# A hybrid block whose second-norm rows are turned in 32x32 squares by VectorE and placed by DMA

## The reference, cut to what matters

```python
x = x + jnp.einsum('bse,ed->bsd', y, w_out[l])

h = rmsnorm(x, norm_ffn[l])
f = jax.nn.silu(jnp.einsum('bsd,df->bsf', h, w_gate[l])) * jnp.einsum('bsd,df->bsf', h, w_up[l])
x = x + jnp.einsum('bsf,fd->bsd', f, w_down[l])
return rmsnorm(x, norm_final)
```

## Time and profile before

| | |
|---|---|
| median of 3 runs | 1905.11 us (1903.91 to 1905.77) |
| span of the profiled execution | 1902.7 us (the profile gives no time beyond it) |
| PE busy | 1875.1 us, 99% |
| DVE, ACT, POOL busy | 1106.6, 808.4, 1144.9 us |
| mean granted clock of PE | 0.996 |
| DMA queue of SP | 283.25 MB, 44.8% of 16 engines |

### The profile page before, as it was taken

One profiled execution on the slowest core, in us unless ns is written; L12 is line 12 of the kernel. 1 busy time (PEld: TensorE's weight loads), 2 busy tenths in 40 slices (PEclk: granted clock), 3 DMA queues, 4 the chain that ended last, 5 costly groups with the idle time before them and its releaser, 6 DMA issues.

```text
span 1902.7 us, 22499 instructions
## 1 busy us (share of the span) xinstructions
PE 1875.1 (99%) x8374; PEld 1544.2 (81%) x8374; DVE 1106.6 (58%) x1269; ACT 808.4 (42%) x938; POOL 1144.9 (60%) x427
## 2 busy tenths in 40 slices
PE   9999999999999999999999999999999999999998
PEld 7888788877788788888888788888888888888886
DVE  6899988997645755455545854445443025433535
ACT  6466766585643533333333433333333222232235
POOL 3577477945734465666655755555555676676663
PEclk9999999999999999999999999999999999999999
DMA  6222132265777334533355433323333765655455
GB/s 196 78 79 88 45 100 78 75 224 172 247 240 231 117 125 127 153 119 127 112 153 176 151 105 114 106 88 105 115 105 127 288 225 190 210 189 211 166 198 221
DMA packets 240946, 284.20 MB, mean 149 GB/s; under 512 B 12095, under 2 KB 166207, under 8 KB 240364
## 3 DMA queue, kind: packets, MB, share of 16 engines
q1 hardware_dynamic: 240874, 283.25, 44.8%
q10 hardware_dynamic: 2, 0.00, 0.0%
HBM read 200.90 MB, written 82.31 MB: 149 GB/s over the span
## 4 chain that ended last, share of the span: by engine, by line
PE 82%; POOL 6%; DVE 5%; ACT 2%; issue 2%; DMA 2%; POOLq 0%; SPq 0%; DVEq 0%; ACTq 0%
PE ps L2133 19%; PE ps L2135 19%; PE ps L2134 19%; PE acc L2133 8%; PE acc L2135 8%; PE acc L2134 8%; DVE a_lo L1863 1%; POOL nsq L877 1%; PE ps L2161 1%; DVE t_sum L1887 1%; POOL nsq L879 1%; POOL w_lo L804 1%; POOL f_lo L1018 0%; DVE wo_lo L1707 0%; POOL glu L827 0%
## 5 line engine op out<-in xcount | busy, mean ns | idle before, releaser
L933 POOL TENSOR_TENSOR t_lo<-t_sum,t_hi 128x2048 fp32r<-128x2048 f32 x44 | 205.6, 4674 | 165.3 <-ACT t_hi L1366 165.2
L927 POOL TENSOR_TENSOR b_lo<-m_raw,b_hi 128x1536 fp32r<-128x1536 f32 x44 | 157.6, 3582 | 179.2 <-ACT b_hi L1361 121.9
L1018 POOL TENSOR_TENSOR f_lo<-f_raw,f_hi 128x2048 fp32r<-128x2048 f32 (+1 forms) x42 | 182.2, 4338 | 129.3 <-ACT f_hi L1518 124.8
L2133 PE MATMUL ps<-h_hi,w_hi 128*128 128x512 f32 x512 | 201.1, 393 | 0.8 <-POOL w_lo L804 0.8
L2135 PE MATMUL ps<-h_hi,w_lo 128*128 128x512 f32 x512 | 199.4, 389 | 0.0
L2134 PE MATMUL ps<-h_lo,w_hi 128*128 128x512 f32 x512 | 199.2, 389 | 0.0
L1887 DVE TENSOR_TENSOR t_sum<-m_raw 128x512 f32<-128x512 f32 x88 | 141.7, 1630 | 97.4 <-PE acc L2135 87.6
L1518 ACT CAST f_hi<-f_raw 128x2048 fp32r<-128x2048 f32 (+1 forms) x42 | 74.3, 1769 | 263.6 <-PE ps L2135 168.1
L2133 PE MATMUL ps<-wd_hi,f_hi 128*128 128x512 f32 x462 | 179.8, 389 | 0.8 <-POOL wd_lo L1025 0.8
L2134 PE MATMUL ps<-wd_lo,f_hi 128*128 128x512 f32 x462 | 179.7, 389 | 0.0
L2135 PE MATMUL ps<-wd_hi,f_lo 128*128 128x512 f32 x462 | 179.7, 389 | 0.0
(11 more groups left out here) (257 smaller groups left out, 4689.1 us busy)
## 6 DMA issues: line engine op xcount, KB each, us to landing
f_raw<-f_scr SPq DMA_DIRECT2D x35, 1024.0 KB, 4.9
wd_raw<-in_w_down SPq DMA_DIRECT2D x60, 512.0 KB, 6.6
f_scr<-fs SPq DMA_DIRECT2D x110, 256.0 KB, 2.1
m_raw<-in_w_gate SPq DMA_DIRECT2D x88, 256.0 KB, 3.9
m_raw<-in_w_up SPq DMA_DIRECT2D x88, 256.0 KB, 5.1
w_raw<-in_w_in SPq DMA_DIRECT2D x32, 512.0 KB, 5.3
f_scr<-gt SPq DMA_DIRECT2D x44, 256.0 KB, 2.0
xt<-in_x SPq DMA_DIRECT2D x16, 512.0 KB, 6.3
```

The lines of the kernel that those rows point to most:

```text
L927: g.tensor_tensor(b_lo[b][:, :, :, :], m_raw[b][:, 0:3], f32(b_hi[b][:, :, :, :]), ALU.subtract).then_inc(s_mlo, 1)
L933: g.tensor_tensor(t_lo[b][:, :, :, :], t_sum[b][:, :, :, :], f32(t_hi[b][:, :, :, :]), ALU.subtract).then_inc(s_mlo, 1)
L1018: g.tensor_tensor(f_lo[j % 3][:, 0:n], f_raw[j % 2][:, 0:n], f32(f_hi[j % 3][:, 0:n]), ALU.subtract).then_inc(s_dlo, 1)
L2133: pe.matmul(bank, lhs[0](c), rhs[0](c), start=first, stop=False, skip_group_check=more)
```

## The change

PE turns nothing any more. DVE's `transpose` turns each 32x32 square of the row in place: 16 instructions `row_turned`, from `hn` into `h2t`. That leaves the squares in the wrong places: square (t, b), for positions 32t to 32t+31 and channels 32b to 32b+31, has its channels on partitions 32t to 32t+31. Four DMAs per row, one for each 32 partitions, bring the squares to their places in DRAM in pieces of 32 numbers (128 B). ACT's queue issues them (`store_h2`), where SP's issued one DMA per row with pieces of 512 B. `h2_scr` has a new layout, and so each load of a quarter is four loads of 32 partitions with pieces of 2 KB as before (`load_quarter`; the quads likewise). `h2t` has four buffers for the first eight rows. DVE waits for a buffer's stores before it turns into it again; ACT waits for the turn before it issues.

```diff
-    h2_scr = nc.dram_tensor("h2_scr", [NH, P, KD, HALF], F32).ap()
+    h2_scr = nc.dram_tensor("h2_scr", [NH, SQ, KD, SQS, HALF], F32).ap()
...
-            def store_h2(w):
-                h, i = divmod(w, TPH)
-                sp_.wait_ge(s_h2c, 2 * (w + 1))
-                sp_.dma_start(h2_scr[h, :, :, i * P:(i + 1) * P], h2t[w % 2][:, :, :]).then_inc(s_h2st[w % 2], 16)
...
+            def load_quarter(n, h, a, done):
...
+                for q in range(SQS):
+                    sp_.dma_start(a_raw[n][q * SQ:(q + 1) * SQ],
+                                  h2_scr[h, :, half * KH:(half + 1) * KH, q, st * TILE:(st + 1) * TILE]).then_inc(done, 16)
...
-            def h2_copy(w):
-                if w == 0:
-                    act.wait_ge(s_wlo, FIRST_APART + PPAIRS + WOQ)
-                elif w >= 2:
-                    act.wait_ge(s_h2st[w % 2], 16 * (w // 2))
-                for b in range(2):
-                    act.wait_ge(s_tr[b], w + 1)
-                    a.copy(h2t[w % 2][:, 4 * b:4 * b + 4], ps[6 + b].rearrange("p (k s) -> p k s", k=4)
-                           ).then_inc(s_h2c, 1)
+            def store_h2(w):
+                h, i = divmod(w, TPH)
+                act.wait_ge(s_turned, w + 1)
+                for t in range(SQS):
+                    a.dma_start(h2_scr[h, :, :, :, i * P + t * SQ:i * P + (t + 1) * SQ].rearrange("j k q s -> j (k q) s"),
+                                h2t[hb(w)][t * SQ:(t + 1) * SQ]).then_inc(s_h2st[hb(w)], 16)
...
+            def row_turned(w):
+
+                dve.wait_ge(s_hn, w + 1)
+                if w >= 4:
+                    dve.wait_ge(s_h2st[hb(w)], h2_stores(hb(w), w))
+                v.transpose(h2t[hb(w)].rearrange("p b i -> p (b i)"), hn[w % 2][:, :]).then_inc(s_turned, 1)
...
-            def turn_h2(w):
-                pe.wait_ge(s_hn, w + 1)
-                for b in range(2):
-                    if w:
-                        pe.wait_ge(s_h2c, 2 * (w - 1) + b + 1)
-                    else:
-                        pe.wait_ge(s_nstd if b == 0 else s_rsty, 2)
-                    for k in range(4):
-                        c = (4 * b + k) * P
-                        mm = pe.transpose(ps[6 + b][:, k * P:(k + 1) * P], hn[w % 2][:, c:c + P], ident[:, :])
-                    mm.then_inc(s_tr[b], 1)
```

More of the change, by code:

```diff
@@ L301, in hybrid_block @@
         s_xr = [sem(f"residual_loaded{n}") for n in range(4)]
-        s_tr = [sem(f"turned{b}") for b in range(2)]
         s_std2 = sem("std2_ready")
         s_hn = sem("hn_ready")
-        s_h2c = sem("h2_copied")
-        s_h2st = [sem(f"h2_stored{n}") for n in range(2)]
+        s_turned = sem("hn_squares_turned")
+        s_h2st = [sem(f"h2_stored{n}") for n in range(4)]
         s_x2st = [sem(f"x2_stored{n}") for n in range(2)]
@@ L418, in from_sbuf, with hb, h2_stores @@
             return m, nd[m][:, :, first * P:(first + 1) * P]
+        def hb(w):
+            return w % 4 if w < TPH else w % 2
+        def h2_stores(n, rows):
+            return 16 * SQS * sum(hb(w) == n for w in range(rows))
         def decay_of(u):
@@ L647, in _ @@
                 if w == LOAD_AT:
-                    for n in range(2):
-                        sp_.wait_ge(s_h2st[n], 16 * TPH // 2)
+                    for n in range(4):
+                        sp_.wait_ge(s_h2st[n], h2_stores(n, TPH))
                     sp_.wait_ge(s_out[3], TPH)
@@ L653, in _ @@
                     for n, a in (((6, "A22"), (5, "A21")), ((1, "A11"), (0, "A12")))[w - LOAD_AT]:
[L654 removed]
+                        load_quarter(n, 0, a, s_a0)
                 if w == LOAD_AT + 2:
@@ L663, in _ @@
                 sp_.dma_start(x2_scr[w], row[w % 4][:, :]).then_inc(s_x2st[w % 2], 16)
-            for w in (NT - 2, NT - 1):
-                store_h2(w)
             def load_quad(k):
-                for n, a in enumerate(("A11", "A12", "A21", "A22")):
-                    sp_.dma_start(quad[:, n], quarter(1, a)[:, k]).then_inc(s_qld, 16)
+                for n, (half, st) in enumerate(((0, 0), (1, 0), (0, 1), (1, 1))):
+                    for q in range(SQS):
+                        sp_.dma_start(quad[q * SQ:(q + 1) * SQ, n],
+                                      h2_scr[1, :, half * KH + k, q, st * TILE:(st + 1) * TILE]
+                                      ).then_inc(s_qld, 16)
             def store_quad(k):
@@ L703, in _ @@
                     if i == QUADS[0]:
-                        for n in range(2):
-                            sp_.wait_ge(s_h2st[n], 16 * NT // 2)
+                        for n in range(4):
+                            sp_.wait_ge(s_h2st[n], h2_stores(n, NT))
                     if i - 1 in QUADS:
@@ L1374, in _ @@
                     row_std(1)
-                    norm_swish(1, between=DIRECT[1], turned=0)
-                    h2_copy(1)
+                    norm_swish(1, between=DIRECT[1])
                 if 4 <= w < NT - 1:
@@ L1402, in _ @@
                     row_std(w)
-                if 5 <= w < NT - 1:
-                    h2_copy(w - 1)
+                for turned in TURNED.get(w, (w - 1,) if 5 <= w < NT - 1 else ()):
+                    store_h2(turned)
                 if 1 < w < NT - 1:
@@ L1482, in gate_block @@
                 sums_hi(m + 1, 1)
-                if starts == 0:
-                    h2_copy(NT - 1)
                 silu(i, 1, h)
                 silu(i, 2, h)
+                if starts == 0:
+                    for w in (NT - 2, NT - 1):
+                        store_h2(w)
                 copy_y(m + 1, i, 1)
@@ L2023, in matrix_block @@
                 sum22(m, i, b, h, first)
+                if first and not b:
+                    row_turned(NT - 2)
+                    row_turned(NT - 1)
                 for n in late:
@@ L2370, in _ @@
                     norm_var(1, 6)
-                for turned in TURNED.get(w, (w - 1,) if 5 <= w < NT - 1 else ()):
-                    turn_h2(turned)
             BANKS = [[ps[4], ps[5], ps[0], ps[5], ps[0], ps[5], ps[5]], [ps[4], ps[1], ps[0], ps[1], ps[0], ps[1], ps[1]]]
```

42 lines of the change are left out of this document (20 added, 22 removed).

## The result

The changed kernel takes 1934.1 us (median; 1930.9 to 1935.3), the kernel before 1904.6 in the same measurement: a ratio of 1.0149, 95% interval 1.0134 to 1.0163. That is some 28 us slower by the ratio and 29.5 by the medians. The forecast was 1909.7 us, slower, with a range that ended at 1924.

A forecast was written before the change was run, and what follows sets the result against it. It started from PE, busy 99% of the span, but expected waits to use up the saving: +0.6 us for the rows, +2.5 and +1.5 for split loads, +4.6 on 1905.1, so 1909.7 us; range 1898 to 1924.

The forecast's parts named there:

- PE's turns: On PE, 16 turned rows at 0.87 us each, plus 0.8 us waiting for ACT's copies: 14.7 us removed.
- DVE's turn: On DVE, 16 added transposes of 128x1024, taken at 1.2 us each.
- The packet of 128 B: In the DMA engines, a 128 B packet taken at 14 ns, bounds 14 and 29.4: 3.6 us a row against 1.9.
- ACT's issues: On ACT, 64 added DMA issues: 6.0 us for eight, 2.8 for four.
- The chain of rows 3 to 9: ACT's issues delay statistics: row 4's 4.2 us later, row 8's +6.1; waits use up PE's nine spared turns.
- my sign of 551: Trace sign for the forecast: the statistics of row 8 on ACT near 551 us.
- Rows 10 and 11: No norm step there, DVE and ACT wait for PE: PE gains 1.7 us, from +1.6 to -0.1 at row 12.
- The loads: Loads of turned rows split in four land later: +2.5 us in the first half, +1.5 in the second.
- Rival 3: Split loads into 32 partitions run at half speed, DVE's first sum waits: 1913.7 us, chance 0.20.
- Rival 4: Small stores or the turn are slow; at 29.4 ns a packet ACT stands 15 us in eight issues: 1925, chance 0.14.
- the sign towards it: Trace sign for Rival 4: a gap over 8 us in ACT, between the squares and row 4's statistics.

The follow-up runs named there:

- e1: Kernel before, but no engine turns the rows; SP stores each row with one DMA of 512 B packets, loads whole: 1897.1 us, ratio 0.9957.
- e2: e1 plus DVE turning each row; SP still stores it with one DMA of 512 B packets, loads whole: 1901.3 us, ratio 0.9978.
- e8: e2 with ACT in place of SP issuing the one 512 B-packet store of a row: 1897.9 us, ratio 0.9954.
- e6: Changed kernel with SP issuing the four 128 B-packet stores of a row, and whole loads: 1907.1 us, ratio 1.0005.
- e3: e2 with each load of turned rows split into four DMAs of 32 partitions: 1909.8 us, ratio 1.0028.
- e4: Changed kernel with SP instead of ACT issuing the four stores of a row, loads still split: 1916.1 us, ratio 1.0055.
- e5: Changed kernel with another scratch order, so each load of turned rows is one DMA into 128 partitions: 1930.6 us, ratio 1.0129.
- e9: Changed kernel with ACT's four stores of a row in packets of 512 B instead of 128 B, loads split: 1911.3 us, ratio 1.0023.
- e12: e5 with ACT's four stores of a row in packets of 256 B instead of 128 B: 1910.7 us, ratio 1.0028.
- e11: e5 with two of a row's four stores issued by ACT and two by SP: 1911.5 us, ratio 1.0020.
- e10: Kernel before, PE still turning, with ACT instead of SP issuing the one 512 B-packet store of a row: 1908.2 us, ratio 1.0010.

## Why the prediction was wrong

The sign was right and the size was not: +4.6 against +28.

- *PE's turns*, 14.7 us: measured 8.2 when nothing takes their place (e1). That the others have next to nothing in hand was right.
- *DVE's turn*, 1.2 us: 1.245. The duration was right; the kernel loses 4.0 by it with SP as the issuer (e2), and e8, with the turn and ACT's one store, is level with e1.
- *The packet of 128 B*, 14 ns: 11.8. The straight line through the earlier trace rows was good enough.
- *ACT's issues*, 6.0 us for eight and 2.8 for four: **this term failed.** Measured 11.65 and 12.46 for eight; 4 to 6 for four where SP's row traffic runs, 10.89 and 15.71 beside the a_raw loads, and 2.77 only alone. I had the evidence: 4.14 us for a store behind others stood in my bounds, and at the worst place it was 3.9 an issue. I took 0.78 an issue from four loads of weights instead, where I should have asked how fast a row's 4096 packets leave the queue. The price is no constant of the issue: with the same stores it moves from 2.77 to 15.71 us, with what the other queue is moving.
- *The chain of rows 3 to 9* had the right links and the wrong lengths: row 4's statistics end at 506.3 and not at 496.6, 13.8 us later than before and not 4.2; those of row 8 begin at 556.35, 14.0 later and not 6.1 (my sign of 551 did not fit that sum, which gives 548.4). *Rows 10 and 11*, where I had PE gaining 1.7 us because ACT and DVE waited for PE, are where the other half is lost: the stores of rows 8 and 9 meet the loads, and the statistics of row 10 begin at 593.16 (before 566.84; in e6, with the same packets on SP, 561.84).
- *The loads*, +4.0: 9.5 with SP's stores (e3 against e2, e4 against e6), 3.8 in the changed kernel, where other things are later still. The second pair was to go out earlier than 568.26; it goes out at 576.98, since SP now waits for DVE's scaled row (71.4 us over 440 to 720), which waits for ACT. At the change of halves ACT waits 7.43 us for a_raw (before 3.43, with whole loads 2.47 in e5):

```profile
1066.81 1.90 ACT L1357 CAST a_hi<-a_raw 128x2048 fp32r<-128x2048 f32 x1 [7.43 <-DMA a_raw<-h_scr]
```

- *Rival 3* (half rate) was true as a mechanism, beside the main one and not in its place. *Rival 4* had the right place (ACT's issues on the chain, from about 5 us a row; it was 5.9) for a wrong reason, since its packets were to be slow by themselves. ACT's 11.65 and 12.46 us are over the 8 us that I had given as the sign towards it.

The loss along e1, e8, e5 and the changed kernel: -8.2 for the work taken away, -0.6 for DVE's turn and ACT's one store in place of SP's, +33.4 for four stores of 128 B packets in place of one of 512 B, +3.8 for the split loads: +28.4. What stays open: whether the room in a queue counts DMAs or packets (for 2048 packets e9's eight DMAs took 8.27 and 6.70 us, e12's four 4.57 to 5.44 beside the loads, e11's two 1.30 to 1.79, there with as many more in SP's queue, so the number of DMAs seems to count as well), and the 5 us by which e6 falls behind e2. No version with the reference's order of data beat the kernel before; e6 is level with it.

## What to carry to other kernels

In these traces a DMA that an engine issues costs it 0.5 to 1.3 us for the first one or two; beyond that the engine stood for up to 7.6 us an issue, and beside a queue of large packets the small ones left at nearly the rate of the large ones. So count the packets of a store before giving it to an engine that computes, look for the longest stretches of issue rather than the median, and put stores of many small packets in the queue behind which the least urgent work stands; SP's was that here, and it still cost 5 us. Where an engine's issue, a statistic and a scaling form a circle over the rows, compare the circle's length with the bound engine's time per row, not the engine's busy share: ACT was busy 41%.

## What the runs showed of the hardware that I had not expected

- The same 4096 packets of 128 B held ACT 2.8 us with free DMA engines and 15.7 us beside the other queue's loads. With the other queue's loads whole (11.6 and 12.0 us) and cut from packets of 2 KB to 512 B, it was 6.2 to 7.9 us, although there were four times as many of them.
- Packets of 128 B took 11.8 ns each, less than half of the 29.4 ns of those of 512 B; a packet of 128 B written to memory cost no more than the straight line through longer ones gives (14 ns).
- Four loads into 32 partitions each moved 205 to 260 GB/s together where one into 128 moved 380 to 410.
- One store of 512 B packets a row, issued by ACT in the middle of its work, was cheaper by 4.6 us than by SP with DVE's turn (e8 against e2, on two chips), and dearer by 1.9 us with PE's turn (e10).
